# Tail table first, and the early expert's second down half behind the tails' up product, in a fused transformer layer

## What is computed

```python
t = rms_norm(h, norm_moe_g).reshape(B * S, D)
g_prob = softmax(t @ w_group + b_group); g_idx = argmax(g_prob)
e_prob = softmax((t @ w_router + b_router) of the chosen group)
top_p, top_i = lax.top_k(e_prob, 2)
weights = g_w * top_p / sum(top_p)
for e in range(16):
    he = silu(t @ w_gate[e]) * (t @ w_up[e])       # 1024 -> 512
    moe = moe + gates[:, e:e+1] * (he @ w_down[e]) # 512 -> 1024
h = h + moe
```

## Time and profile before

| | us |
|---|---|
| median of 3 runs | 1386.47 |
| lowest and highest run | 1383.16 and 1386.52 |
| the profiled execution, its own time | 1386.29 |
| its span, first to last instruction | 1384.3 |
| PE busy in the span | 1322.6 (96%) |
| ACT and DVE busy | 740.3 and 840.1 |
| granted TensorE clock, mean | 0.990 of full speed |

### The profile page before, as it was taken

How to read it: one execution, slowest core, us unless ns; L and a number is a source line. 1 busy time by engine, 2 the same in 40 slices (tenths; PEclk the granted TensorE clock), 3 DMA queues, 4 the chain that set the end, 5 groups by cost and what they waited for, 6 DMA issues and landing times.

```text
span 1384.3 us, 21736 instructions
## 1 busy us (share of the span) xinstructions
PE 1322.6 (96%) x8200; PEld 993.5 (72%) x8200; DVE 840.1 (61%) x1664; ACT 740.3 (53%) x1422; POOL 150.4 (11%) x236
## 2 busy tenths in 40 slices
PE   6999999999999989999999999999989999999995
PEld 5888998844445745455887887787767888888884
DVE  5523124647666977675777533334746787787876
ACT  6321176546657756666334334333325677776765
POOL 1000000012240030000000000000035222221211
PEclk9999999999999989999999999999999999999998
DMA  7141113441000030102113010000667999999993
GB/s 240 24 168 46 65 62 122 183 167 51 1 1 1 1 122 1 62 31 79 59 46 138 0 60 32 31 31 31 219 250 202 327 371 330 348 343 333 363 337 111
DMA packets 89218, 186.46 MB, mean 135 GB/s; under 512 B 14094, under 2 KB 25266, under 8 KB 88370
## 3 DMA queue, kind: packets, MB, share of 16 engines
q1 hardware_dynamic: 80050, 166.11, 33.4%
q0 software_dynamic: 7008, 19.28, 5.7%
q10 hardware_dynamic: 2080, 0.01, 0.1%
HBM read 165.45 MB, written 25.56 MB: 138 GB/s over the span
## 4 chain that ended last, share of the span: by engine, by line
PE 79%; DVE 8%; DMA 5%; ACT 4%; issue 2%; POOL 1%; DVEq 0%; ACTq 0%; SPq 0%; POOLq 0%
PE psum L2503 29%; PE psum L2754 19%; PE psum L2646 7%; PE psum L2669 5%; PE psum L2487 5%; PE psum L2628 4%; DMA up_stage<-in_w_up 4%; PE psum L2480 3%; PE psum L2979 3%; PE psum L2988 1%; PE psum L2910 1%; DVE up_rest L1996 1%; PE psum L2966 1%; ACT arena L1448 1%; ACT up_high L1471 1%
## 5 line engine op out<-in xcount | busy, mean ns | idle before, releaser
L1136 ACT ACTIVATE arena<-psum 128x512 f32<-128x512 f32 (+3 forms) x195 | 85.7, 493 | 83.9 <-PE psum L2669 46.2
L2646 PE MATMUL psum<-arena 64*128 64x512 f32 (+7 forms) x384 | 116.2, 521 | 7.8 <-ACT arena L1429 5.7
L1874 DVE TENSOR_TENSOR_SCAN arena<-arena,singles 128x768 f32<-128x768 f32 (+7 forms) x64 | 86.4, 1364 | 53.7 <-POOL arena L933 47.5
L2646 PEld LDWEIGHTS psum<-arena 64*128 64x128 f32 (+1 forms) x384 | 49.2, 190 | 75.3 <-issue 50.5
L2669 PEld LDWEIGHTS psum<-ident,arena 128*128 128x128 f32 x576 | 65.4, 143 | 51.5 <-ACT arena L1136 25.4
L2487 PE MATMUL psum<-arena 128*128 128x512 f32 (+2 forms) x280 | 93.8, 488 | 0.8 <-DVE arena L1855 0.8
L2669 PE MATMUL psum<-ident,arena 128*128 128x128 f32 x576 | 84.6, 283 | 8.5 <-DVE arena L1874 4.4
L2480 PE MATMUL psum<-ident,arena 128*128 128x128 f32 (+1 forms) x520 | 74.0, 280 | 19.6 <-ACT arena L1154 9.4
L1996 DVE TENSOR_TENSOR down_rest<-down_stage,down_high 128x1024 fp32r<-128x1024 f32 x60 | 71.4, 1220 | 26.8 <-ACT down_high L1471 26.8
L2480 PEld LDWEIGHTS psum<-ident,arena 128*128 128x128 f32 (+1 forms) x520 | 59.9, 140 | 35.5 <-issue 17.5
L2628 PE MATMUL psum<-arena 128*64 128x512 f32 (+3 forms) x384 | 83.5, 515 | 0.0
(11 more groups left out here) (566 smaller groups left out, 3415.3 us busy)
## 6 DMA issues: line engine op xcount, KB each, us to landing
gate_stage<-in_w_gate SPq DMA_DIRECT2D x16, 2048.0 KB
up_stage<-in_w_up SPq DMA_DIRECT2D x16, 2048.0 KB
down_stage<-in_w_down SPq DMA_DIRECT2D x15, 2048.0 KB, 9.2
arena<-in_x SPq DMA_DIRECT2D x16, 512.0 KB, 3.6
arena<-in_w_mkv SPq DMA_DIRECT2D x8, 1024.0 KB, 6.1
arena<-in_w_in SPq DMA_DIRECT2D x4, 1024.0 KB, 10.6
arena<-in_w_mo SPq DMA_DIRECT2D x4, 1024.0 KB, 6.5
mv_times_w_mo_spill<-arena SPq DMA_DIRECT2D x8, 512.0 KB, 3.2
```

Source lines behind the costliest of these rows:

```text
L1136: do(act.activation(dst, src, ACT.Copy), s_te["act"])
L1874: do(dve.tensor_tensor_scan(w_row(u, r, a)[:, 0:L][:, ::-1], f_sb[:, n % FAILS, 0:L][:, ::-1], tiny.to_broadcast([P, L]), 1.0, ALU.mult, A ...
L2646: mm = pe.matmul(scores_of(kind, n)[:, at:end], lhs, rhs(at, end), start=True, stop=True)
```

## The change

DVE reads the tail table before it makes the first half of the slot table's operands, not behind it. On PE the slot table's product is cut in two halves of 8 steps, with the turning of the tails' rows between them, and `early_down(1)` moves from inside the slot table's product to behind `rows_in(START)`. ACT's `output 1` follows to behind the tails' silu and `high(START, 0)`, and `high(START, 1)` is no longer cut in two around the tails' output. No instruction of the computation is added or dropped; one wait of PE (for `output 1`) goes.

```diff
-PE_DID = counted("early ranks", "early tokens", "rows turned 0", "rows turned 1", "gate", "up", "hidden turned", "down 0", "down 1",
-                 "tail rows turned", "tail gate", "tail up", "tail hidden turned", "tail down")
-ACT_DID = counted("rows 0", "rows 1", "silu", "hidden", "tail rows", "output 0", "output 1", "tail silu", "tail hidden", "tail output")
+PE_DID = counted("early ranks", "early tokens", "rows turned 0", "rows turned 1", "gate", "up", "hidden turned", "down 0",
+                 "tail rows turned", "tail gate", "tail up", "down 1", "tail hidden turned", "tail down")
+ACT_DID = counted("rows 0", "rows 1", "silu", "hidden", "tail rows", "output 0", "tail silu", "output 1", "tail hidden", "tail output")
...
-            act.wait_ge(s_ed, DVE_DID["shares"])
-            for half in range(2):
+            def early_output(half):
                 act.wait_ge(s_ep, PE_DID[f"down {half}"])
...
+            act.wait_ge(s_ed, DVE_DID["shares"])
+            early_output(0)
             act.wait_ge(s_ep, PE_DID["tail gate"])
...
             high(START, 0)
+            early_output(1)
             act.wait_ge(s_ep, PE_DID["tail hidden turned"])
...
             rows_high(START)
-            high(START, 1, (0, 1))
             act.wait_ge(s_ep, PE_DID["tail down"])
...
-            high(START, 1, (2, 3))
+            high(START, 1)
...
+            tail_places()
             slot_tables(0)
-            tail_places()
             slot_tables(1)
...
             early_down(0)
-            table(range(T // 2))
-            early_down(1)
-            table(range(T // 2, 2 * T)).then_inc(s_tab, 1)
+            table(range(T))
...
             mm.then_inc(s_ep, 1)
+            table(range(T, 2 * T)).then_inc(s_tab, 1)
             pe.wait_ge(s_ea, ACT_DID["tail rows"])
             tail_rows_by(early_w[0], bank(2), EARLY_TAILS).then_inc(s_ep, 1)
             pe.wait_ge(s_ed, DVE_DID["shares"])
             tail_rows_by(early_w[1], bank(3), EARLY_TAILS).then_inc(s_ep, 1)
             pe.wait_ge(s_te["dve"], EMPTIED[ROUND[("rank", 0, 0)]][1])
             rows_in(START)
+            early_down(1)
             pe.wait_ge(s_ed, DVE_DID["tail hidden"])
...
             pe.wait_ge(s_ea, ACT_DID["tail hidden"])
-            pe.wait_ge(s_ea, ACT_DID["output 1"])
             tail_down(EARLY_TAILS, early_w[2], 6).then_inc(s_ep, 1)
```

## The result

The change is slower. Median 1398.3 us (1395.45 to 1400.98, 5 runs) against 1385.02 us (1383.16 to 1386.52, 5 runs) of the kernel before on the same chip; the ratio is 1.0084, with a 95% interval of 1.0065 to 1.0102. Measured again later it was 1396.96 against 1386.1 us, ratio 1.0082 (1.0063 to 1.0100). The profiled execution took 1395.45 us with a span of 1393.4.

A forecast was written before the change was run, and what follows sets the result against it. PE's progress from the early hidden product to START's tail gate at 1051.15 us was taken to bound the kernel. Terms -1.6 - 1.9 + 3.3 + 1.5 gave +1.3 us: 1387.8 on the median, range 1384.0 to 1391.6.

The forecast's parts named there:

- the wait for ACT's copies: PE, ahead of START's tail gate, waits for copies queued behind ACT's rounding of the later up weights: +1.5 us.
- the up load: START's up weights, issued behind the moved down half at about 1038, take 9.5 us with POOL's gathers between.
- the piece that I named: From the early slot's hidden product (1011.5 us) to START's tail gate (1051.15); PE's gain or loss there passes on one to one.
- start of the tails' gate: Earlier gathers and the table's second half behind the turning start the tails' gate at 1022.8, not 1024.43: -1.6 us.
- tails' gate and up: The 1.90 us pause in the tails' gate goes because the up weights are loaded only afterwards: -1.9 us.
- tails' down starts later: The down half, now uncovered behind the tails' up product, delays the tails' down on PE: +3.3 us.
- Landing of the gathers: The last tail gather, issued at 1017.15, lands at 1020.7, bounds 1019.85 and 1023.85: 1.85 us gained.
- The rule that I had set beside it: DMA engines alternate between queues packet by packet, so the tail gathers would land near 1019.9, 0.8 us better.
- the pause goes: -1.9: The stop in the tails' gate, taken for instructions arriving late behind the up load, disappears: -1.9 us.
- rival 4: START's up load takes 13.32 us, ACT rounds late and PE waits 5.3 us: +5.1 us, 1391.6; chance 0.08.
- U + 17: 17 us after the tails' up product ends; up_high waiting beyond it would show the forecast wrong.
- my rival with rows that come no earlier: The last tail gather takes 6.0 us and the gate starts at 1025.3: +3.8 us in all, 1390.3; chance 0.09.

The follow-up runs named there:

- the kernel with the load behind the gate: Tail table first and rows turned inside the table's product, early_hT moved, START's up load issued after the tails' gate, rounding undivided, against the kernel before: 1383.92 us, ratio 0.9987.
- tail table first: The kernel before with one edit, DVE reading the tail table ahead of the slot table's operands: 1385.07 us, ratio 0.9994 to the kernel before.
- down half back: The changed kernel with early_down(1) at its old place inside the table's product and ACT in the old order: 1384.33 us, ratio 0.9987 to the kernel before.
- both cures: The changed kernel with the first down half multiplied twice and START's up load issued behind the tails' rows turned: 1388.25 us, ratio 1.0023 to the kernel before.
- the kernel with the wait filled: The changed kernel with the first down half multiplied twice, to occupy PE before the tails' rows land: 1392.39 us, ratio 1.0043 to the kernel before.

## Why the prediction was wrong

I forecast +1.3 us (1387.8) and got +10.9 to +13.3. Two steps failed: the wait for ACT's copies was put at 1.5 us and was 5.2, because the up load was put at 9.5 us and took 13.44; and the lowered clock behind PE's new waits, 4.4 us, was left at nothing. All of it is in the piece that I named, and it is passed on one to one as I said; the terms failed. In the piece:

| term | predicted | measured | how |
|---|---|---|---|
| start of the tails' gate | -1.6 | +0.4 | 1024.26 - 1011.01 = 13.25 against 12.89 |
| tails' gate and up | -1.9 | -0.4 | 12.59 against 13.01 |
| tails' down starts later | +3.3 | +3.4 | 1042.47 - 1036.85 = 5.62 against 1039.62 - 1037.44 = 2.18 |
| wait for ACT's copies | +1.5 | +5.2 | the list of waits |
| tails' products of `START` | 0 | +1.4 | 8.69 against 7.26 |

With 0.1 us of small differences this is the +10.1.

**Landing of the gathers.** I took 1020.7 and had 1019.85 to 1023.85 as bounds. The last gather was issued when I said (5.61 us behind the early hidden product, as forecast) and landed 4.62 us later, not the 3.55 that I took. The landing gained 0.8 us, not 1.85. Being issued inside a load costs a gather about 2 us here (4.62 against the 2.67 of the earlier trace rows). The rule that I had set beside it (the Trainium skill, "DMA: Bandwidth & Descriptors", arbitration), read as no delay at all, was further off than my sum.

**The clock, which I left out.** I wrote that PE would wait "some 2 us" ahead of the rows, and then costed every step behind it at the durations of the earlier trace rows, which are those of full clock. The wait was 3.6 us, the clock fell to 0.50 behind it, and the turning and the table's half took 2.99 us (1021.27 to 1024.26) where the same steps took 1.83 us at full clock (1021.58 to 1023.41, the kernel with the load behind the gate). The gate and up took 12.59 us where they take 10.78 without a pause at full clock. So the clock took 1.2 and 1.8 us, and behind the second wait 1.4 us more: 4.4 us in the profiled execution, for which I had nothing. This term was missing, and it is what "the pause goes: -1.9" was paid with: the pause did go.

**The up load.** This was my rival 4, at a chance of 0.08: 13.32 us and a wait of 5.3 us. The measured values are 13.44 and 5.2. By the sign that I had set, `up_high` waiting beyond U + 17, I was wrong too: it began at U + 17.95 (1054.80 - 1036.85). I gave it little because the 13.32 us of the loop is for two loads at once and "here it is one". I counted POOL's gathers as company for the load, and left out the additions of the early slot, of which I had written that they cost nothing since POOL has time. POOL has; the DMA engines have not. The run with the additions held back shows them at 2.9 us. The 8.8 us that I started from were also misread as a load alone: beside that load run the additions of a tail (from 1070.73) and, from 1073.62, the next gate load. The two up loads with only a row gather beside them took 9.4 and 9.6 us, so the 9.5 that I took for a load with all its gathers is what one takes nearly without; with them it was 10.55.

**The down half** was sized rightly (3.4 against 3.3), and my rival with rows that come no earlier was nearly true at the gate but for another reason.

What stays open: the changed kernel's runs lie some 1.5 us further above before than the two profiled pieces, and in the first measurement 3 us. Its runs show a mean granted clock of 0.983 to 0.987, those of before, beside the second measurement, 0.988 to 0.993, so a part of it may be clock lost in runs that were not profiled; no trace shows where.

## What to carry to other kernels

Before a product is moved out of a stretch in which its engine would otherwise wait, ask twice what it covered: there it was free, and with it PE was at work and the clock at 1.00, where without it the clock read 0.50 behind the wait. What stands behind a new wait of PE has to be costed at both levels of the clock. And look at what is released by the step that moves: here a 2 MB load hung on it by an overlap of buffers, it moved by 20 us into the company of POOL's row additions, and it cost more than all that was moved on PE; 512 words in another place would have unhooked it.

## What the hardware showed beyond that

The pause of 1.90 us ("issue") in a dense stream of small products depends on a weight load in flight: 1.90, 1.09, 1.11 and 1.04 us in the kernels with the load issued ahead of the gate (before, tail table first, down half back, both cures), and none at that place with it issued behind the gate. It comes at the same product each time. The lowered clock falls mostly on the work behind a wait, so that 3 us of products done twice made the whole program faster than leaving PE idle. A gather of 128 rows of 1 KB issued near the end of a weight load landed 4.0 to 4.8 us from its issue, and one issued at a load's start 6.9 to 7.4 us (`START`'s tails in the kernel with the wait filled, in the change measured again and in the one with the additions held back), against 2.7 to 2.9 with free engines.
